# A decoder layer on one core: query and latent-key projections computed with features on partitions, cross scores kept in the row buffer, a norm in two steps, and a last recurrence level by products

## The chip, the core and the metric

One NeuronCore of one Trainium2 chip. The metric is device time in microseconds for one execution of the whole kernel. All arithmetic is f32; large products are made of three f32r matmuls each (high by high, high by low, low by high).

## The reference, cut to what matters

256 tokens, width 2048, one layer. Cut to the parts near the change:

```python
hq, hf, hi, hg, cq, ckv, kr, gate_a, gate_b = split(h @ w_in)
# gated linear recurrence, 16 heads of 128
q = silu(hq);  f = lb + (1 - lb) * sigmoid(hf);  k = 1 - f;  v = hi
o = hgrn2_chunked(q, k, v, log(f))     # o_t = S_t^T q_t,  S_t = diag(f_t) S_(t-1) + k_t^T v_t
o = rmsnorm(o, g_hg_out) * silu(hg)
y_a = o @ w_o_hg
# latent attention, 16 heads, 128 plain and 64 rotary features
q_m = rmsnorm(cq, g_q_lora) @ w_uq;   kv = rmsnorm(ckv, g_kv_lora) @ w_ukv
att = causal_softmax_attention([q_nope, rope(q_rope)], [k_nope, rope(kr)], v_m)
y_b = att @ w_o_mla
merged = sigmoid(gate_a) * y_a + sigmoid(gate_b) * y_b
y = merged @ w_out                      # then norms, residual, SwiGLU, norms, residual
```

## The kernel before, in words

**Stages.** A start phase (to about 277 us) makes the modulated input hT and the latents cT, both transposed (features on partitions) and split in high and low parts. Then a loop over 4 groups of 4 heads (512 columns). Then three 2048-column projections (attention output "om", recurrence output "oh", "out"), and the channel mixing over 11 blocks of 512 hidden columns.

**Chunks.** All weights stream in chunks of 2 x 128 rows by 512 columns (512 KB) through a ring of 4 slots. For chunk c, SP issues the load into `raw` when the low part of chunk c - 4 is done; ScalarE rounds it to `whi` (line 463) when chunk c - 4 is multiplied; VectorE makes `wlo` = raw - whi (line 1220); TensorE multiplies (lines 836 to 838): 2 token tiles x 2 row tiles x 3 products, the activations as the stationary operand and the weights moving, into one of two pairs of PSUM banks. The remaining four banks are the workspaces XA (banks 4, 5) and XB (6, 7).

**The turn.** The group loop is software pipelined and written out by hand over the step t. In a turn i, TensorE multiplies the chunks t = 0 to 7 (values of the recurrence, HI) and 8 to 15 (output gate, HG) of group i, then for group i + 1: t = 16, 17 the query (UQ), 18, 19 the latent key (UK), 20, 21 the rotary query (UR, 256 columns), 22, 23 the value (UV), 24 to 31 the forget gate (HF), 32 to 39 the recurrence query (HQ). Each engine runs over the same t, ScalarE and VectorE up to three chunks ahead of TensorE, and after its chunk work it does what `recur` (group i) and `attention` (group i + 1) have for that t. The first group's attention runs alone ("lead", t from 16), the last group's recurrence runs in a tail: t = 0 to 15, then beside the chunks c of "om", with t = 16 + c.

**Recurrence.** With qT, kT (features on partitions) and bT (running sums of log f), the scores are made level by level, LEVELS = 64, 32, ..., 1. For a level of half length m, POOL subtracts bT at the middle of each block of 2m (`differences`, lines 197, 198), ScalarE exponentiates the tile in place (596), VectorE multiplies the later halves with qT and the earlier halves with kT into zT (1503, 1504), TensorE multiplies each of 8 head tiles with itself (981, t = DECAY[L] - 2, so t = 15 for the last), and VectorE merges the result into pT by a mask (1517). POOL's last difference (193) is for the scores between the two token tiles: TensorE 990 (t = 16), ScalarE's copy to pTx (601, t = 19), which is the first half of qT. Then TensorE's `attend` (862 to 864, t = 18) gives the outputs in XB. ScalarE squares them (607, t = 21). VectorE at t = 20 multiplies the gate (1536), which frees the bank pair that chunk 18 needs, and at t = 22 it reduces the squares (1540), makes mean + eps, waits for POOL's power (789), normalises (1544) and gates (1549).

**Attention.** The query of 16, 17 comes out with tokens on partitions; ScalarE copies it to `stage` (t = 20), TensorE transposes it into XA (845, t = 21), ScalarE copies it to qT (617, t = 24). The key goes through `v` (t = 22), TensorE (t = 24, after the norm has left XB), and to kT (623, t = 27). VectorE rotates the rotary query at t = 23 (1380 to 1386), TensorE transposes it at t = 25 (1014). The scores follow at t = 27 (1026, 1027), softmax, and `attend` at t = 35. `stage` holds the forget gate from t = 35.

**Beside it.** Half-chunks of the modulation matrix are accumulated by VectorE (`ada_piece`, line 1227) at the steps in ADA_TURN, and in "om" at c = 4, 5, 7, 8, 9, 10, 13, ...; SP loads two ahead. In the tail, finished rows are transposed by TensorE (854), raised by ScalarE (`rows_high`, 573) and lowered by VectorE (`rows_low`, 1440 or 1437); chunk c of "om" needs the rows c.

Of the kernel before, what the change touches and what calls it, by code (L numbers as in the profile page):

```python
# [114 lines left out]
def build(nc, x, vectors, consts, masks, positions, ada0, ada1, ada2, ga_bias, post_rows, w_start, w_kr, w_uqn, w_uqr, w_uk, w_uv, w_hf,  # L115
          w_hq, w_hi, w_hg, w_omla, w_ohg, w_out, w_gate, w_up, w_down, out):
    ctx = ExitStack()
    with ctx:
# [29 lines left out]
        pTx = qT[:, 0:HPG]  # L148
        v = sb("v", [P, TT, NW])
# [37 lines left out]
        def differences(eng, L):  # L187
# [7 lines left out]
            b, d = halves(flat(bT), m), halves(d, m)  # L195
            end = b[:, :, 0, m - 1:m].broadcast_to([P, HPG * P // m, m])
# [109 lines left out]
        T_CROSS, T_SUM, T_OG, T_OSQ, T_ON = DECAY[-1] - 2, DECAY[-1], 20, 21, 22  # L306
# [149 lines left out]
        def _(act):  # L456
# [118 lines left out]
            def recur(pl, t, g):  # L575
# [10 lines left out]
                if t + 1 in DECAY:  # L586
# [8 lines left out]
                    dif = tiles(dec[:, L % 2])[:, :, 0, :] if L == len(LEVELS) else dec[:, L % 2]  # L595
# [3 lines left out]
                if t == DECAY[-1] + 1:  # L599
                    act.wait_ge(sig("cross_scored"), g + 1)  # L600
                    nc.scalar.activation(pTx, by_tile(XB)[:, HPG:], ACT.Copy).then_inc(sig("cross_copied"), 1)
# [7 lines left out]
            def attention(pl, t, g, back):  # L609

                if t == 20:
                    from_pair(pl, I_UQ, T_UK - 1, stage[:])
                if t == 22:
                    from_pair(pl, I_UK, T_UR - 1, v[:])
                if t == 24:
                    act.wait_ge(sig("q_transposed"), g + 1)
                    nc.scalar.activation(qT[:], by_tile(XA), ACT.Copy).then_inc(sig("qT_copied"), 1)
                if t == 26:
                    act.wait_ge(sig("k_transposed"), g + 1)
                    from_pair(pl, I_UV, T_HF - 1, v[:])  # L620
                if t == 27:
                    act.wait_ge(sig("k_transposed"), g + 1)
                    nc.scalar.activation(kT[:], by_tile(XB), ACT.Copy).then_inc(sig("kT_copied"), 1)
# [195 lines left out]
        def _(pe):  # L819
# [20 lines left out]

            def transpose_group(src, bank):
# [16 lines left out]
            def attend():  # L858

                for h in range(HPG):  # L860
                    cols = slice(h * P, (h + 1) * P)
                    nc.tensor.matmul(PS[:, XB, cols], pT[:, 2 * h], v[:, 0, cols], start=True, stop=True)
                    nc.tensor.matmul(PS[:, XB + 1, cols], pTx[:, h], v[:, 0, cols], start=True, stop=False)
# [75 lines left out]
            def mix(pl, t):  # L939
# [5 lines left out]
                elif t < T_HF:  # L945
                    i, c = divmod(t - T_UQ, CL)
                    j = i % 2
                    if c == 0:
                        pe.wait_ge(sig("c_low"), j + 1)
                    multiply(pl, I_UQ + i, CL, T_UQ + i * CL, c, c + 1, cT_hi[:, j], cT_lo[:, j],  # L950
                             NW // 2 if I_UQ + i == I_UR else NW)
# [4 lines left out]
            def recur(pl, t, g):  # L956
# [13 lines left out]
                if t + 2 in DECAY[:-1]:  # L970
# [9 lines left out]
                    for i in range(2 * HPG):  # L980
# [12 lines left out]
                if t == T_SUM:  # L993
                    pe.wait_ge(sig(f"level{len(LEVELS) - 1}_merged"), g + 1)
                    pe.wait_ge(sig("cross_copied"), g + 1)
                    attend().then_inc(sig("o_summed"), 1)

            def attention(pl, t, g, back, total):

                if t == 21:  # L1000
                    pe.wait_ge(sig("krT_copied"), 1)
# [895 lines left out]
```

## Time and profile before

| | |
|---|---|
| median of 3 runs | 1898.57 us (1896.83 to 1901.4) |
| the profiled execution's own time | 1899.58 us |
| its span, first to last instruction | 1897.8 us |
| mean granted TensorE clock | 0.991 of full |
| TensorE busy | 1830.3 us (96%) |
| chain that ended last | TensorE 57%, issue 29%, POOL 5%, VectorE 5%, DMA 4%, ScalarE 1% |
| HBM | 423.38 MB by DMA, 223 GB/s in the mean |

Everything comes from one profiled execution. A listed matmul duration reaches from its start to its modelled end and overlaps the next one; the distance between starts is what a matmul costs the queue. In the timeline an f32 matmul that runs in two passes is counted twice ("x16" for 8 instructions). "Idle before" is time in which the engine did nothing, with what ended it. Names: PE is TensorE, PEld its weight loads, DVE VectorE, ACT ScalarE, SP the queue that issues the DMAs.

### The profile page before, as it was taken

To read this page: it belongs to the slowest core of one execution; us is meant where nothing else is said; L and a number is where in the kernel's file an instruction comes from. 1 tells how busy PE (TensorE), PEld (TensorE's weight loads), DVE (VectorE), ACT (ScalarE), POOL (GpSimd) and SP (SyncE) were. 2 spreads that over 40 slices of the span, in tenths; PEclk is the share of its full clock that TensorE was granted. 3 is DMA by queue.
4 is the path that set the end of the run, shared out by engine and by line. 5 is a ranking of instruction groups with operands and counts; after the bars stand their busy time and mean duration, and the time that the engine had idled before them with its cause. 6 is when DMAs were issued, how large, how long until landed. Compare 5 with 4: busy or idle time off the path is not lost.

```text
span 1897.8 us, 24442 instructions
## 1 busy us (share of the span) xinstructions
PE 1830.3 (96%) x8884; PEld 1536.2 (81%) x8884; DVE 1295.4 (68%) x1361; ACT 893.0 (47%) x1007; POOL 107.4 (6%) x76
## 2 busy tenths in 40 slices
PE   3999999999999999999999998999999999999997
PEld 2788888888888888887878877888888888888886
DVE  7899768668668667677677545566656666665557
ACT  5544545645645645644334446444443444343443
POOL 0000000120120120120000000000000000000000
PEclk9999999999999999999999998999999999999999
DMA  9997548646646646546787653666666666665553
GB/s 384 409 363 249 193 160 291 231 156 227 227 155 222 231 155 222 198 148 239 257 309 245 221 189 105 237 223 221 215 233 222 211 226 220 231 210 177 190 191 131
DMA packets 115985, 423.38 MB, mean 223 GB/s; under 512 B 13008, under 2 KB 13392, under 8 KB 115408
## 3 DMA queue, kind: packets, MB, share of 16 engines
q1 hardware_dynamic: 115920, 422.51, 63.4%
q8 instruction: 42, 0.69, 0.1%
q14 instruction: 23, 0.19, 0.0%
HBM read 420.36 MB, written 2.10 MB: 223 GB/s over the span
## 4 chain that ended last, share of the span: by engine, by line
PE 57%; issue 29%; POOL 5%; DVE 5%; DMA 4%; ACT 1%; SPq 0%; POOLq 0%; DVEq 0%; ACTq 0%
PE PS L836 18%; PE PS L838 18%; PE PS L837 18%; POOL dec L197 3%; DMA ada_raw<-in_ada 2%; DVE ada_acc L1227 2%; POOL dec L198 2%; DMA raw<-in_w_start 2%; DVE wlo L1220 1%; PE PS L871 1%; PE PS L1138 1%; PE PS L845 1%; PE PS L896 0%; POOL dec L193 0%; PE PS L854 0%
## 5 line engine op out<-in xcount | busy, mean ns | idle before, releaser
L1220 DVE TENSOR_TENSOR wlo<-raw,whi 128x1024 fp32r<-128x1024 f32 x600 | 731.9, 1222 | 421.8 <-ACT whi L463 420.0
L463 ACT ACTIVATE whi<-raw 128x1024 fp32r<-128x1024 f32 x600 | 630.0, 1053 | 741.1 <-PE PS L838 671.9
L836 PE MATMUL PS<-whi,hT_hi 128*128 128x512 f32 x1792 | 708.5, 395 | 11.2 <-DVE wlo L1220 4.3
L838 PE MATMUL PS<-whi,hT_lo 128*128 128x512 f32 x1792 | 699.5, 390 | 0.0
L837 PE MATMUL PS<-wlo,hT_hi 128*128 128x512 f32 x1792 | 699.0, 390 | 0.0
L836 PEld LDWEIGHTS PS<-whi,hT_hi 128*128 128x128 f32 x1792 | 337.6, 188 | 82.4 <-issue 5.3
L838 PEld LDWEIGHTS PS<-whi,hT_lo 128*128 128x128 f32 x1792 | 337.1, 188 | 71.3
L837 PEld LDWEIGHTS PS<-wlo,hT_hi 128*128 128x128 f32 x1792 | 337.7, 188 | 67.6 <-issue 0.2
L836 PE MATMUL PS<-whi,cT_hi 128*128 128x512 f32 (+1 forms) x592 | 230.9, 390 | 4.9 <-DVE wlo L1220 3.4
L838 PE MATMUL PS<-whi,cT_lo 128*128 128x512 f32 (+1 forms) x592 | 227.9, 385 | 0.0
L837 PE MATMUL PS<-wlo,cT_hi 128*128 128x512 f32 (+1 forms) x592 | 227.7, 385 | 0.0
L1227 DVE SCALAR_TENSOR_TENSOR ada_acc<-ada_raw,csilu,ada_acc 128x512 f32<-128x512 f32 (+1 forms) x185 | 141.2, 763 | 35.4 <-DMA ada_raw<-in_ada 31.8
L836 PEld LDWEIGHTS PS<-whi,cT_hi 128*128 128x128 f32 x592 | 111.7, 189 | 29.2 <-DVE wlo L1220 5.3
L838 PEld LDWEIGHTS PS<-whi,cT_lo 128*128 128x128 f32 x592 | 111.6, 188 | 22.5
L837 PEld LDWEIGHTS PS<-wlo,cT_hi 128*128 128x128 f32 x592 | 111.8, 189 | 21.2
L789 POOL TENSOR_TENSOR stat<-stat,con 128x2 f32<-128x2 f32 (+2 forms) x11 | 12.9, 1175 | 1336.9 <-DVE stat L1279 1321.5
L1392 DVE TENSOR_TENSOR gate<-gate,PS 128x1024 f32<-128x1024 f32 x64 | 78.0, 1219 | 14.5 <-PE PS L838 14.3
L197 POOL TENSOR_TENSOR dec<-bT 128x512 f32<-128x512 f32 x28 | 54.0, 1929 | 413.4 <-DVE bT L1485 338.9
L981 PEld LDWEIGHTS PS<-zT 128*128 128x128 f32 x448 | 54.0, 191 | 1.9
L981 PE MATMUL PS<-zT 128*128 128x64 f32 x448 | 53.0, 271 | 0.0
L1517 DVE COPY_PREDICATED pT<-msk,PS 128x512 f32<-128x512 uint8 x28 | 25.1, 896 | 37.4 <-issue 30.2
L596 ACT ACTIVATE dec<-dec 128x1024 f32<-128x1024 f32 (+1 forms) x32 | 32.1, 1003 | 21.0 <-POOL dec L198 21.0
(222 smaller groups left out, 1054.8 us busy)
## 6 DMA issues: line engine op xcount, KB each, us to landing
ada_raw<-in_ada SPq DMA_DIRECT2D x142, 512.0 KB, 4.9
raw<-in_w_gate SPq DMA_DIRECT2D x88, 512.0 KB, 4.3
raw<-in_w_up SPq DMA_DIRECT2D x88, 512.0 KB, 4.2
raw<-in_w_down SPq DMA_DIRECT2D x88, 512.0 KB, 4.2
raw<-in_w_start SPq DMA_DIRECT2D x80, 512.0 KB, 5.0
raw<-in_w_hf SPq DMA_DIRECT2D x32, 512.0 KB, 4.2
raw<-in_w_hq SPq DMA_DIRECT2D x32, 512.0 KB, 5.2
raw<-in_w_hi SPq DMA_DIRECT2D x32, 512.0 KB, 4.3
```

The costliest lines, as they stand in the source:

```text
L197: eng.tensor_tensor(d[:, :, 1, :], b[:, :, 1, :], end, ALU.subtract)
L198: return eng.tensor_tensor(d[:, :, 0, :], end, b[:, :, 0, :], ALU.subtract)
L463: nc.scalar.activation(whi[:, pl.slot(c), 0:w], raw[:, pl.slot(c), 0:w], ACT.Copy)\
L596: nc.scalar.activation(dif, dif, ACT.Exp).then_inc(sig("decays"), 1)
L836: nc.tensor.matmul(o, hi[:, kt, tok], whi[:, s, cols], start=start, stop=False)
L837: nc.tensor.matmul(o, hi[:, kt, tok], wlo[:, s, cols], start=False, stop=False)
L838: last = nc.tensor.matmul(o, lo[:, kt, tok], whi[:, s, cols], start=False, stop=stop)
L981: last = nc.tensor.matmul(PS[:, XA + L % 4, i * 64:(i + 1) * 64], z[:, i], zt[:, i, :, 1, :], start=True, stop=True)
L1220: nc.vector.tensor_tensor(wlo[:, s, 0:w], raw[:, s, 0:w], whi[:, s, 0:w].bitcast(F32), ALU.subtract)\
L1227: last = nc.vector.scalar_tensor_tensor(out=acc, in0=slot, scalar=csilu[:, a:a + 1], in1=acc, op0=ALU.mult, op1=ALU.add)
L1392: nc.vector.tensor_tensor(dst, dst, banks(2 * p), ALU.add).then_inc(pair_free[p], 1)
L1517: nc.vector.copy_predicated(o, mask.unsqueeze(1).broadcast_to(shape), PS[:, XA + L % 4, :].rearrange("p (i x m) -> p i x m", i=2 * HPG, m=m))\
```

## The change

- The chunks of UQ and UK are multiplied by a new `multiply_columns`: the weights are the stationary operand and the 256 tokens move, so that the result has the features on partitions. ScalarE copies it straight to qT and kT. The transposes of `stage` and `v` at t = 21 and 24, and the two copies behind them, are gone; their waits are put elsewhere.
- The cross scores of the recurrence go to `crossed`, the first half of `stage`, instead of to the first half of qT.
- The last recurrence level (m = 1) is made of one difference, an exponential of half the size, two products on VectorE, of which the second uses the first, and one matmul with ones.
- The norm of the recurrence output is cut in two: reduce and mean + eps at t = 22, the rest at t = 24.
- In the tail `rows_low` of rows 6 and 7 is at c = 5 instead of c = 6.

```diff
+        crossed = stage[:, 0].rearrange("p (h s) -> p h s", s=P)
...
             b, d = halves(flat(bT), m), halves(d, m)
+            if m == 1:
+                return eng.tensor_tensor(dec[:, L % 2, 0:NW], b[:, :, 1, 0], b[:, :, 0, 0], ALU.subtract)
...
-        T_CROSS, T_SUM, T_OG, T_OSQ, T_ON = DECAY[-1] - 2, DECAY[-1], 20, 21, 22
+        T_CROSS, T_SUM, T_OG, T_OSQ, T_OMEAN, T_ON = DECAY[-1] - 2, DECAY[-1], 20, 21, 22, 24
...
@@ ScalarE, recur @@
-                    dif = tiles(dec[:, L % 2])[:, :, 0, :] if L == len(LEVELS) else dec[:, L % 2]
+                    dif = (tiles(dec[:, L % 2])[:, :, 0, :] if L == len(LEVELS) else
+                           dec[:, L % 2, 0:NW] if LEVELS[L] == 1 else dec[:, L % 2])
                     nc.scalar.activation(dif, dif, ACT.Exp).then_inc(sig("decays"), 1)
...
-                    nc.scalar.activation(pTx, by_tile(XB)[:, HPG:], ACT.Copy).then_inc(sig("cross_copied"), 1)
+                    nc.scalar.activation(crossed, by_tile(XB)[:, HPG:], ACT.Copy).then_inc(sig("cross_copied"), 1)
@@ ScalarE, attention @@
                 if t == 20:
-                    from_pair(pl, I_UQ, T_UK - 1, stage[:])
+                    if back is not None:
+                        act.wait_ge(sig("decayed"), back * 8 + 8)
+                    from_pair(pl, I_UQ, T_UK - 1, flat(qT))
                 if t == 22:
-                    from_pair(pl, I_UK, T_UR - 1, v[:])
-                if t == 24:
-                    act.wait_ge(sig("q_transposed"), g + 1)
-                    nc.scalar.activation(qT[:], by_tile(XA), ACT.Copy).then_inc(sig("qT_copied"), 1)
+                    from_pair(pl, I_UK, T_UR - 1, flat(kT))
                 if t == 26:
-                    act.wait_ge(sig("k_transposed"), g + 1)
+                    if back is not None:
+                        act.wait_ge(sig("o_summed"), back + 1)
                     from_pair(pl, I_UV, T_HF - 1, v[:])
-                if t == 27:
-                    act.wait_ge(sig("k_transposed"), g + 1)
-                    nc.scalar.activation(kT[:], by_tile(XB), ACT.Copy).then_inc(sig("kT_copied"), 1)
@@ TensorE @@
+            def multiply_columns(pl, g, c0, c, hi, lo):
+
+                p = pl.pair(g)
+                if c == 0 and not pl.fresh(g):
+                    pe.wait_ge(pair_free[p], pl.freed(g))
+                pe.wait_ge(lo_ready, pl.through(c0 + c))
+                s = pl.slot(c0 + c)
+                for h in range(HPG):
+                    o = PS[:, 2 * p + h // 2, h % 2 * T:(h % 2 + 1) * T]
+                    for k in range(KC):
+                        kt = c * KC + k
+                        cols = slice(k * NW + h * P, k * NW + (h + 1) * P)
+                        start, stop = c == 0 and k == 0 and h % 2 == 0, c == CL - 1 and k == KC - 1
+                        nc.tensor.matmul(o, whi[:, s, cols], hi[:, kt, :], start=start, stop=False, skip_group_check=True)
+                        nc.tensor.matmul(o, whi[:, s, cols], lo[:, kt, :], start=False, stop=False, skip_group_check=True)
+                        last = nc.tensor.matmul(o, wlo[:, s, cols], hi[:, kt, :], start=False, stop=stop,
+                                                skip_group_check=True)
+                last.then_inc(multiplied, 1)
...
+                    if I_UQ + i in (I_UQ, I_UK):
+                        multiply_columns(pl, I_UQ + i, T_UQ + i * CL, c, cT_hi[:, j], cT_lo[:, j])
+                    else:
+                        multiply(pl, I_UQ + i, CL, T_UQ + i * CL, c, c + 1, cT_hi[:, j], cT_lo[:, j],
+                                 NW // 2 if I_UQ + i == I_UR else NW)
@@ TensorE, recur @@
-                    for i in range(2 * HPG):
+                    if m == 1:
+                        last = nc.tensor.matmul(PS[:, XA + L % 4, :], ones, zT[:, L % 2, NW:2 * NW], start=True, stop=True)
+                    for i in range(2 * HPG if m > 1 else 0):
@@ TensorE, attention @@
-                if t == 21:
-                    pe.wait_ge(sig("krT_copied"), 1)
-                    pe.wait_ge(pair_free[pl.pair(I_UQ)], pl.freed(I_UQ) + 1)
-                    transpose_group(stage, XA).then_inc(sig("q_transposed"), 1)
-                if t == 24:
-                    if back is not None:
-                        pe.wait_ge(sig("o_normed"), back + 1)
-                    pe.wait_ge(pair_free[pl.pair(I_UK)], pl.freed(I_UK) + 1)
-                    transpose_group(v, XB).then_inc(sig("k_transposed"), 1)
-                    pe.wait_ge(sig("qT_copied"), g + 1)
...
                 if t == 27:
 
-                    pe.wait_ge(sig("kT_copied"), g + 1)
+                    if back is not None:
+                        pe.wait_ge(sig("o_normed"), back + 1)
+                    pe.wait_ge(sig("krT_copied"), 1)
+                    pe.wait_ge(pair_free[pl.pair(I_UQ)], pl.freed(I_UQ) + 1)
+                    pe.wait_ge(pair_free[pl.pair(I_UK)], pl.freed(I_UK) + 1)
                     pe.wait_ge(sig("qrT_copied"), g + 1)
@@ VectorE, recur @@
+                    if L == len(LEVELS) - 1:
+                        later, products = zT[:, L % 2, 0:NW], zT[:, L % 2, NW:2 * NW]
+                        nc.vector.tensor_tensor(later, halves(flat(qT), 1)[:, :, 1, 0], dec[:, L % 2, 0:NW], ALU.mult)\
+                          .then_inc(sig("q_stepped"), 1)
+                        dve.wait_ge(sig("q_stepped"), g + 1)
+                        nc.vector.tensor_tensor(products, halves(flat(kT), 1)[:, :, 0, 0], later, ALU.mult)\
+                          .then_inc(sig("decayed"), 1)
+                        return
...
-                if t == T_ON:
+                if t == T_OMEAN:
...
-                    rsqrt_of(stat[:, 32:40], P, "o", g)
+                    nc.vector.tensor_scalar(stat[:, 32:40], stat[:, 32:40], 1.0 / P, EPS, ALU.mult, ALU.add)\
+                      .then_inc(sig("o_mean"), 1)
+                if t == T_ON:
+
+                    dve.wait_ge(sig("o_rsqrt"), g + 1)
...
-                for u in {3: (4, 5), 6: (6, 7), 12: (8, 9), 14: (10, 11), 29: (12,), 30: (13,), 31: (14,), 32: (15,)}.get(c, ()):
+                for u in {3: (4, 5), 5: (6, 7), 12: (8, 9), 14: (10, 11), 29: (12,), 30: (13,), 31: (14,), 32: (15,)}.get(c, ()):
```

## Rows read from the trace of the kernel before

**Rows 1.** The page: engines (part 1), modulation products (part 5), their loads (part 6).
```profile
PE 1830.3 (96%) x8884; PEld 1536.2 (81%) x8884; DVE 1295.4 (68%) x1361; ACT 893.0 (47%) x1007; POOL 107.4 (6%) x76
...
L1227 DVE SCALAR_TENSOR_TENSOR ada_acc<-ada_raw,csilu,ada_acc 128x512 f32<-128x512 f32 (+1 forms) x185 | 141.2, 763 | 35.4 <-DMA ada_raw<-in_ada 31.8
...
ada_raw<-in_ada SPq DMA_DIRECT2D x142, 512.0 KB, 4.9
```

**Rows 2.** Who waited for whom, TensorE, 370 to 512.4 us (one turn).
```profile
PE PS L836 <- DVE wlo L1220: 1.2, 2, 1.0
```

**Rows 3.** The same view, 797.2 to 900 us (the last group's recurrence).
```profile
PE PS L836 <- DVE hT_lo L1440: 3.7, 1, 3.7
```

**Rows 4.** Timeline, TensorE, one turn: start us, us, engine, line, operation [idle before].
```profile
408.97 0.39 PE L836 MATMUL PS<-whi,hT_hi 128*128 128x512 f32 x1
...
411.69 1.89 PE L981 MATMUL PS<-zT 128*128 128x64 f32 x16
...
416.25 1.07 PE L990 MATMUL PS<-zT 128*128 128x128 f32 x8
...
420.57 0.49 PE L836 MATMUL PS<-whi,cT_hi 128*128 128x512 f32 x1 [0.48 <-DVE side L1536]
...
428.83 0.28 PE L836 MATMUL PS<-whi,cT_hi 128*128 128x256 f32 x1
...
431.70 1.04 PE L845 MATMUL PS<-con,stage 128*128 128x128 f32 x8
...
435.12 0.39 PE L838 MATMUL PS<-whi,cT_lo 128*128 128x512 f32 x1
436.48 0.50 PE L836 MATMUL PS<-whi,cT_hi 128*128 128x512 f32 x1 [0.97 <-DVE wlo L1220]
...
442.64 1.03 PE L845 MATMUL PS<-con,v 128*128 128x128 f32 x8
...
446.25 0.60 PE L1014 MATMUL PS<-con,zT 128*128 128x128 f32 x4
```

**Rows 5.** Timeline, TensorE's weight loads, a rotary chunk.
```profile
288.50 0.19 PEld L836 LDWEIGHTS PS<-whi,cT_hi 128*128 128x128 f32 x1
```

**Rows 6.** Timeline, TensorE, in the channel mixing.
```profile
1729.51 3.60 PE L1163 MATMUL PS<-gate,con 128*128 128x512 f32 x8
...
1733.18 0.39 PE L837 MATMUL PS<-wlo,hT_hi 128*128 128x512 f32 x1
```

**Rows 7.** Timeline, VectorE, the same turn.
```profile
410.68 0.68 DVE L1504 TENSOR_TENSOR zT<-kT,dec 128x512 f32<-128x512 f32 x1
...
429.44 1.21 DVE L1540 TENSOR_REDUCE stat<-dec 128x8 f32<-128x1024 f32 x1
...
432.60 1.23 DVE L1544 TENSOR_TENSOR dec<-PS,stat 128x1024 f32<-128x1024 f32 x1 [1.75 <-POOL stat L789]
434.07 1.23 DVE L1549 TENSOR_TENSOR mixed<-dec,side 128x1024 f32 x1 [0.24 <-DVE dec L1544]
435.21 1.22 DVE L1220 TENSOR_TENSOR wlo<-raw,whi 128x1024 fp32r<-128x1024 f32 x1
...
438.46 2.36 DVE L1220 TENSOR_TENSOR wlo<-raw,whi 128x1024 fp32r<-128x1024 f32 x2
```

**Rows 8.** Timeline, VectorE, the last group's output norm.
```profile
864.90 1.23 DVE L1544 TENSOR_TENSOR dec<-PS,stat 128x1024 f32<-128x1024 f32 x1 [1.75 <-POOL stat L789]
```

**Rows 9.** Timeline, TensorE, the same stretch.
```profile
863.99 0.39 PE L838 MATMUL PS<-whi,hT_lo 128*128 128x512 f32 x1
868.04 0.50 PE L836 MATMUL PS<-whi,hT_hi 128*128 128x512 f32 x1 [3.66 <-DVE hT_lo L1440]
...
875.25 0.39 PE L836 MATMUL PS<-whi,cT_hi 128*128 128x512 f32 x1
```

**Rows 10.** Busy times, 868.4 to 871.6 us; the granted clock stands before DMA share, GB/s.
```profile
868.40:871.60 3.20, 3.20 (x9) 2.50 (x8) 3.17 (x5) 0.00 (x0) 0.00 (x0) 0.52 0.24 77
```

**Rows 11.** Timeline, ScalarE, the same stretch.
```profile
858.53 1.09 ACT L573 ACTIVATE hT_hi<-PS 128x512 fp32r<-128x512 f32 x2 [2.15 <-PE PS L854]
```

More of the change, by code:

```diff
@@ L856, in transpose_pair, with attend @@
                 return last
-            def attend():
+            def attend(across):
                 for h in range(HPG):
@@ L862, in attend @@
                     nc.tensor.matmul(PS[:, XB, cols], pT[:, 2 * h], v[:, 0, cols], start=True, stop=True)
-                    nc.tensor.matmul(PS[:, XB + 1, cols], pTx[:, h], v[:, 0, cols], start=True, stop=False)
+                    nc.tensor.matmul(PS[:, XB + 1, cols], across[:, h], v[:, 0, cols], start=True, stop=False)
                     last = nc.tensor.matmul(PS[:, XB + 1, cols], pT[:, 2 * h + 1], v[:, 1, cols],
@@ L949, in mix @@
                         pe.wait_ge(sig("c_low"), j + 1)
-                    multiply(pl, I_UQ + i, CL, T_UQ + i * CL, c, c + 1, cT_hi[:, j], cT_lo[:, j],
-                             NW // 2 if I_UQ + i == I_UR else NW)
+                    if I_UQ + i in (I_UQ, I_UK):
[3 more added lines that the diff above has]
+                                 NW // 2 if I_UQ + i == I_UR else NW)
                 else:
@@ L995, in recur @@
                     pe.wait_ge(sig("cross_copied"), g + 1)
-                    attend().then_inc(sig("o_summed"), 1)
+                    attend(crossed).then_inc(sig("o_summed"), 1)
             def attention(pl, t, g, back, total):
-                if t == 21:
-                    pe.wait_ge(sig("krT_copied"), 1)
-                    pe.wait_ge(pair_free[pl.pair(I_UQ)], pl.freed(I_UQ) + 1)
-                    transpose_group(stage, XA).then_inc(sig("q_transposed"), 1)
-                if t == 24:
-                    if back is not None:
-                        pe.wait_ge(sig("o_normed"), back + 1)
-                    pe.wait_ge(pair_free[pl.pair(I_UK)], pl.freed(I_UK) + 1)
-                    transpose_group(v, XB).then_inc(sig("k_transposed"), 1)
-                    pe.wait_ge(sig("qT_copied"), g + 1)
                 if t == 25:
@@ L1039, in attention @@
                     pe.wait_ge(sig("p_copied"), g * 2 + 2)
-                    attend().then_inc(sig("att_summed"), 1)
+                    attend(pTx).then_inc(sig("att_summed"), 1)
                 if t == 39:
```

## The prediction

> **What bounds the kernel now.** First the page's engine totals: TensorE is busy 96% of the span, VectorE 68%, ScalarE 47% [rows 1]. So what counts is whether an edit shortens TensorE's own queue, or a wait of TensorE. Then who waited for whom, for TensorE, around the parts touched. In one turn of the group loop it waits three times: twice for a low part of a weight chunk (wlo, L1220), once for the output gate (side, L1536) [rows 2, 4]. In the last group's recurrence it waits once, for the low rows of L1440, 3.7 us [rows 3]. Then TensorE's timeline, where the start-to-start distance of matmuls is the price of each, since the listed durations overlap [rows 4]; and VectorE's timeline, to see why it was late. I number chunks by the loop variable t of a turn.
>
> **The yardstick.** A chunk of 12 matmuls of 512 columns takes 411.69 - 408.97 = 2.72 us, 0.227 each [rows 4]. The sum is made against the profiled execution's own 1899.58 us (span 1897.8); the median of the runs is 1898.57, 1.0 us lower.
>
> **1. Sixteen transposes a group go (t = 21 and 24).** From the start of the q block at 431.70 to the end of the chunk behind it (last matmul 435.12, plus 0.23) is 3.65 us; less the chunk's 2.72, the block costs 0.93. The k block: 446.25 - 442.64 - 2.72 = 0.89 [rows 4]. Together 1.82, the drag on the chunk behind included; four groups: **-7.3 us**. ScalarE loses its two copies of transposed data (L617, L623): it lies beside other work, worth nothing by itself.
>
> **2. Query and key chunks run with 24 matmuls of 256 columns instead of 12 of 512.** The same columns, twice the weight loads. The rotary chunks already have that width: 24 of them take 431.70 - 428.83 = 2.87 us, 0.12 each [rows 4]. So +0.15 a chunk, 4 chunks a group, 16 in all: +2.4. In each turn one of the four (t = 17) runs while TensorE would wait anyhow: the chunk behind it waits 0.48 for the gate at 420.57 [rows 4], which hangs on ScalarE's copy of the cross scores and so on the cross product of 416.25, not on the chunk between. That gives 0.15 back in three turns: **+1.95 us**. A load is listed with 0.19 [rows 5], yet the 256-column matmuls start 0.12 apart, so the loads are overlapped.
> By the gap formula in the Trainium skill (TensorE: Matmul & The Clock Gate, "Back-to-back issue gap": columns at 2.4 GHz plus 2.5 ns) a chunk would grow by an estimated 0.03 us and this term would be 0.5; the row's 0.12 is above that formula's 0.109, and I go by the row.
>
> **3. The last level's eight products become one.** The block of t = 15: 416.25 - 411.69 - 2.72 = 1.84 us [rows 4]. The new instruction (ones against 512 columns of f32) has four of its kind in L1163: 1733.18 - 1729.51 less one matmul of 0.227 is 3.44, 0.86 each [rows 6]; with 0.05 of drag, 0.91. Gain 0.93, four groups: **-3.7 us**. Bounds: no cheaper than one plain pass (0.227, gain 1.6), no dearer than now (gain 0). Around it: POOL makes one difference instead of two and ScalarE half an exponential, both earlier on the chain; VectorE still makes two products of half the tile, but the second now waits for the first. The nearest such wait of VectorE on itself is 0.24 [rows 7]. The product was ready at 410.68 + 0.68 = 411.36 and used at 411.69, so 0.33 covers 0.24; if not, it costs about 0.1 a turn. The input stride of the two products is as before.
>
> **4. The norm in two steps takes VectorE's stall away.** Now VectorE at t = 22 reduces (429.44), stands 1.75 us for POOL's power (432.60), normalises and gates, and only at 435.21 comes to the low part of chunk 23; the rotation then puts that of chunk 24 at 438.46 [rows 7]. TensorE has ended chunk 22 at 435.35 and reaches 442.64 after two chunks: 7.29 - 5.44 = 1.85 us lost, the slower matmuls after each restart included [rows 4]. After the change, on the same clock: parts 2 and 3 shift TensorE by -0.93 + 0.45 = -0.48 before the place where the q block stood, so chunk 22 starts at 431.2 and chunks 23, 24, 25 are wanted at 433.9, 436.7, 439.4. VectorE: reduce and scale to 430.4, low part of 23 (about 1.15; two are 2.36 [rows 7]) ready 431.5, rotation (438.46 - 435.21 less a low part, 2.1) to 433.6, low part of 24 at 434.8; the norm and gate, 2.6 at t = 24 with POOL done long before, to 437.4; low part of 25 at 438.5. The least slack is 0.9. All 1.85 goes, in three turns: **-5.55 us**. The first group has no such waits, because no recurrence runs beside it.
> The moved waits: scores at t = 27 now stand behind the norm (o_normed), ready about 436 and wanted after 445; ScalarE's value copy at t = 26 waits for o_summed, its query copy at t = 20 for the decays, both done earlier on the same chain. While ScalarE held t = 26 for the key transposes, chunk 27's high part stood behind it; that comes earlier now. SP's loads follow the low parts and are not reordered. POOL's order is the same, one instruction shorter.
>
> **5. The tail.** Rows 6 and 7 are lowered at c = 5, ahead of the reduce; before, behind the whole norm, which begins at 864.90 after 1.75 us for POOL [rows 8]. TensorE, which could have gone on at 863.99 + 0.23 = 864.22, starts at 868.04 [rows 9], and after that pause its granted clock is 0.52 of full, that is the 1.2 GHz level, for some 3.2 us [rows 10], so that two chunks end at 875.25 instead of 864.22 + 5.44 = 869.66: 5.59 us lost [rows 9]. Afterwards ScalarE's high rows (858.53 to 859.6 [rows 11]) let VectorE lower rows 6 and 7 by 860.8, do the modulation piece of c = 5 that now stands behind them (two products of 0.76 [rows 1]), and the low part of chunk 6 by 863.5: 0.7 ahead of 864.22. Chunks 7 and 8 have about 1.0. Then norm and gate at c = 8, its modulation piece and the low part of chunk 9 end near 873.6, when TensorE, three chunks and a block of transposes after 864.22, wants it at 873.3; that new wait with its restart is 0.5. **-5.1 us**. The modulation load for c = 8 waits for the piece of c = 5, now at 862.3; it lands 4.9 us later [rows 1] and is used at 871.
>
> **Sum**: -7.3 + 1.95 - 3.7 - 5.55 - 5.1 = -19.7; 1899.6 - 19.7 = 1879.9, and as the median stands 1.0 lower I say 1879.5.
>
> **Rivals.**
> A. VectorE stays late: the norm's second half at t = 24 delays the next chunks as the first did. For it: VectorE's queue is dense there, slack 0.9. Against: the 1.75 stall goes whatever the order. It returns 5.55: 1885. Chance 0.12.
> B. The tail's wait stays, for chunk 6 or 9: VectorE stands at c = 5 for the high rows with the modulation piece and chunk 6's low part queued behind it. If that passes the pause which brought the lower clock, all of 5.1 returns: 1884.6. Chance 0.08; A and B both, 1890, within these.
> C. Slower: the weight loads of the columns form aren't hidden. Its place is the 16 query and key chunks, 192 more loads; it decides at (19.7 + 1.95) / 192 = 0.11 us a load. At the listed 0.19 [rows 5] it is +36.5 in place of +1.95: 1914. Against: the 256-column rows, load included, at 0.12 [rows 4]; new is only which operand is stationary. Chance 0.03.
> The Trainium skill (TensorE: Matmul & The Clock Gate, Part 3, "What overlaps and what doesn't") says that a weight load overlaps running matmuls only when its row group differs. By that rule this rival would be the forecast; the trace disagrees with it.
> D. The change doesn't do what it says: another wait takes back what the queue sheds, so that TensorE stands where it did (time about 1898). TensorE's few waits in a turn speak against. Chance 0.03.
> E. More gain: the single product at one pass and the gate's wait gone too (-2.7 - 1.5): 1875. Chance 0.05.
> The forecast itself: 0.69.
>
> **Numbers.** Range 1874 to 1887: E below, A or B singly above with two microseconds of run-to-run spread; outside are both together, C and D. About 0.2% (3.8 us) is what a measurement of this kernel can tell from no change. Faster 0.94, same 0.03, slower 0.03.
>
> **What would show it.** Right: no transposes from stage or v at t = 21 and 24 (L845's count down by 64); query and key chunks at 2.87 us; one product at the last level, 0.9 us between its neighbours; no wait of TensorE for wlo in a turn, the 0.48 for the gate still there; in the tail no wait above 1 us and a granted clock at full. Wrong: 256-column matmuls 0.19 apart or more (C); a wlo wait at chunks 23 to 26 (A); a TensorE pause over 3 us or a half clock in the tail (B).

## The result and the profile after

The changed kernel takes 1888.57 us (median of 4 runs, 1886.25 to 1891.49), the kernel before beside it 1899.64 (4 runs, 1896.83 to 1901.4). The ratio is 0.9943, with an interval of 0.993 to 0.9957. It is 11.1 us faster. I had said 20: the direction was right, and the time lies 1.6 us outside the range. The profiled execution took 1891.49 us, the slowest of the four, its span is 1889.7 and its mean granted clock 0.987. So the two profiles compared below lie only 8.1 us apart, and the medians 11.1.

From the page of the kernel after, engine totals and DMA queues ([rows 1] answer to the first line). The second fence is the line of the page before for the same queue:

```profile
PE 1828.1 (97%) x8956; PEld 1542.1 (82%) x8956; DVE 1295.1 (69%) x1361; ACT 885.4 (47%) x999; POOL 102.5 (5%) x72
...
q8 instruction: 60, 0.98, 0.2%
```

```profile
q8 instruction: 42, 0.69, 0.1%
```

Who waited for whom, TensorE, whole span, kernel after: in all, times, longest.

```profile
PE PS L837 <- issue: 5.9, 3, 3.0
PE PS L837 <- DVE wlo L1239: 3.3, 5, 0.8
PE PS L891 <- DVE ada_acc L1246: 3.2, 2, 1.9
PE PS L855 <- DVE side L1563: 1.2, 3, 0.4
```

The waits that I had read are gone: none for wlo in a turn [rows 2], none for the low rows in the tail [rows 3]. But there is one that I had not asked for. "Issue" is time in which TensorE waited for nothing that the profile shows; the kernel before has it once, 3.0 us at the start, the kernel after three times, 5.9 us.

TensorE's timeline after, one turn, against [rows 4]. The product block with ones (L1004; "x2", two passes) starts at 411.82, the query chunk (L855 to L857) runs at 0.12 a matmul, the wait for the gate is 0.38, and from the rotary chunk at 428.38 to the rotation's transposes at 442.18 nothing stands between the chunks:

```profile
411.82 1.02 PE L1004 MATMUL PS<-zT,con 128*128 128x512 f32 x2
412.28 0.69 PE L855 MATMUL PS<-cT_hi,whi 128*128 128x256 f32 x1
...
415.31 0.28 PE L856 MATMUL PS<-cT_lo,whi 128*128 128x256 f32 x1
415.43 0.28 PE L857 MATMUL PS<-cT_hi,wlo 128*128 128x256 f32 x1
415.55 1.06 PE L1015 MATMUL PS<-zT 128*128 128x128 f32 x8
...
419.86 0.38 PE L855 MATMUL PS<-cT_hi,whi 128*128 128x256 f32 x1 [0.38 <-DVE side L1563]
...
428.38 0.28 PE L837 MATMUL PS<-whi,cT_hi 128*128 128x256 f32 x1
...
431.26 0.40 PE L837 MATMUL PS<-whi,cT_hi 128*128 128x512 f32 x1
...
442.18 0.60 PE L1029 MATMUL PS<-con,zT 128*128 128x128 f32 x4
```

VectorE's timeline after, the same turn, against [rows 7]. The reduction is followed by the mean and at once by the low part of chunk 23, and the norm comes at 434.99 with no wait for POOL:

```profile
428.85 1.21 DVE L1567 TENSOR_REDUCE stat<-dec 128x8 f32<-128x1024 f32 x1
430.10 0.17 DVE L1570 TENSOR_SCALAR stat<-stat 128x8 f32<-128x8 f32 x1
430.59 1.23 DVE L1239 TENSOR_TENSOR wlo<-raw,whi 128x1024 fp32r<-128x1024 f32 x1 [0.31 <-ACT whi L466]
...
433.85 1.22 DVE L1239 TENSOR_TENSOR wlo<-raw,whi 128x1024 fp32r<-128x1024 f32 x1
434.99 1.22 DVE L1575 TENSOR_TENSOR dec<-PS,stat 128x1024 f32<-128x1024 f32 x1
```

**Where the time went.** I laid the starts of the first matmul of 596 of the 600 chunks (all but the last four, which another line multiplies) of the two profiled executions side by side, in order. Negative is earlier than before; each row is the change of the difference over its stretch:

| stretch (times of before) | change, us |
|---|---|
| start phase, to 90 us (instructions that the change doesn't touch) | +1.24 |
| lead: four column chunks +0.62, transposes -1.75 | -1.1 |
| first turn, up to its end: level -0.85, columns +0.28, transposes -1.79, norm -1.85 | -4.2 |
| **from the first turn's last product to the next turn's second chunk** | **+3.2** |
| second turn | -4.2 |
| **its end and the third turn's beginning** | **+4.4** |
| third turn, and then out of the loop | -4.2 |
| tail: level -0.87, the wait for the low rows and its clock -5.59 | -6.5 |
| attention output and the stages behind it, from 875 us | +3.2 |
| sum | -8.1, as the spans (1897.8 and 1889.7) |

The parts that I had costed bring -20.2 where I had said -19.7. What is missing was lost in places where the change edits nothing, above all at the two jumps back of the loop. TensorE's timeline there, first the kernel before, with the 16 passes of the one-column sums (L871) that end a turn and the next turn's first chunk:

```profile
495.15 1.84 PE L871 MATMUL PS<-con,ada_acc 128*128 128x1 f32 x16
496.86 0.49 PE L836 MATMUL PS<-whi,hT_hi 128*128 128x512 f32 x1
497.18 0.40 PE L837 MATMUL PS<-wlo,hT_hi 128*128 128x512 f32 x1
```

The same in the kernel after, at the first jump, the second, and at the end of the third turn, where the loop is left and nothing jumps:

```profile
491.08 1.84 PE L891 MATMUL PS<-con,ada_acc 128*128 128x1 f32 x16
494.33 0.49 PE L837 MATMUL PS<-whi,hT_hi 128*128 128x512 f32 x1 [1.42 <-issue]
...
495.52 0.63 PE L838 MATMUL PS<-wlo,hT_hi 128*128 128x512 f32 x1
495.95 0.63 PE L839 MATMUL PS<-whi,hT_lo 128*128 128x512 f32 x1
...
632.48 1.84 PE L891 MATMUL PS<-con,ada_acc 128*128 128x1 f32 x16
635.75 0.79 PE L837 MATMUL PS<-whi,hT_hi 128*128 128x512 f32 x1 [1.42 <-issue]
...
775.16 1.84 PE L891 MATMUL PS<-con,ada_acc 128*128 128x1 f32 x16
776.87 0.49 PE L837 MATMUL PS<-whi,hT_hi 128*128 128x512 f32 x1
```

Busy times of the kernel after behind each jump and behind the third turn (PE, PEld, DVE, ACT, POOL, then granted clock, DMA share, GB/s):

```profile
495.00:499.00 4.00, 4.00 (x12) 3.09 (x11) 2.33 (x5) 3.63 (x8) 0.00 (x0) 0.57 0.02 5
...
636.00:641.00 5.00, 5.00 (x12) 3.86 (x13) 2.93 (x7) 4.00 (x8) 0.00 (x0) 0.50 0.12 35
...
775.00:779.00 4.00, 4.00 (x27) 3.60 (x26) 1.02 (x2) 3.61 (x5) 0.00 (x0) 1.00 0.42 134
```

At each jump TensorE stands 1.42 us, and then its granted clock is 0.57 and 0.50, that is mostly the 1.2 GHz level: 8 and 14 matmuls 0.43 us apart instead of 0.227. And what came in meanwhile stands in the instruction queue: DMA queues between 475 and 780 us, before and then after.

```profile
q8 instruction: 1, 0.02, 0.0%
```

```profile
q8 instruction: 19, 0.31, 0.4%
```

These 18 more are all that the page counts more (60 against 42). 0.31 MB in 19 packets is 16 KB each.

### The profile page after: what moved, and what is told of

Same layout as the page of the kernel before. It is cut to its first block, busy times and chain, and to the rows that moved or that the text cites. A ratio compares the mean times of both kernels' runs of the same rounds, so it can differ in the third digit from the quotient of the medians.

```text
span 1889.7 us, 24569 instructions
## 1 busy us (share of the span) xinstructions
PE 1828.1 (97%) x8956; PEld 1542.1 (82%) x8956; DVE 1295.1 (69%) x1361; ACT 885.4 (47%) x999; POOL 102.5 (5%) x72
## 4 chain that ended last, share of the span: by engine, by line
PE 88%; DVE 5%; DMA 4%; issue 1%; ACT 1%; SPq 0%; POOL 0%; DVEq 0%; ACTq 0%; POOLq 0%
PE PS L837 26%; PE PS L839 26%; PE PS L838 26%; DMA ada_raw<-in_ada 3%; DVE ada_acc L1246 2%; PE PS L1006 2%; DMA raw<-in_w_start 1%; PE PS L891 1%; DVE wlo L1239 1%; PE PS L865 1%; PE PS L855 1%; PE PS L856 1%; PE PS L857 1%; PE PS L1046 1%; PE PS L1045 1%
## 5 line engine op out<-in xcount | busy, mean ns | idle before, releaser
L837 PE MATMUL PS<-whi,cT_hi 128*128 128x512 f32 (+1 forms) x528 | 204.4, 387 | 0.5 <-DVE wlo L1239 0.5
L838 PE MATMUL PS<-wlo,cT_hi 128*128 128x512 f32 (+1 forms) x528 | 203.1, 385 | 0.0
L839 PE MATMUL PS<-whi,cT_lo 128*128 128x512 f32 (+1 forms) x528 | 203.0, 384 | 0.0
L837 PEld LDWEIGHTS PS<-whi,cT_hi 128*128 128x128 f32 x528 | 100.0, 189 | 20.2 <-DVE wlo L1239 1.1
L839 PEld LDWEIGHTS PS<-whi,cT_lo 128*128 128x128 f32 x528 | 99.8, 189 | 19.6
L838 PEld LDWEIGHTS PS<-wlo,cT_hi 128*128 128x128 f32 x528 | 99.9, 189 | 18.9
L200 POOL TENSOR_TENSOR dec<-bT 128x512 f32<-128x512 f32 x24 | 44.3, 1845 | 396.2 <-DVE bT L1504 327.3
L1006 PEld LDWEIGHTS PS<-zT 128*128 128x128 f32 x384 | 46.2, 192 | 1.6
L1006 PE MATMUL PS<-zT 128*128 128x64 f32 x384 | 45.4, 271 | 0.0
L1766 DVE SCALAR_TENSOR_TENSOR gate<-ada_raw,csilu,gate 128x1024 f32<-128x1024 f32 x32 | 40.9, 1279 | 0.0
```

The costliest lines, as they stand in the source:

```text
L200: eng.tensor_tensor(d[:, :, 1, :], b[:, :, 1, :], end, ALU.subtract)
L837: nc.tensor.matmul(o, hi[:, kt, tok], whi[:, s, cols], start=start, stop=False)
L838: nc.tensor.matmul(o, hi[:, kt, tok], wlo[:, s, cols], start=False, stop=False)
L839: last = nc.tensor.matmul(o, lo[:, kt, tok], whi[:, s, cols], start=False, stop=stop)
L1006: last = nc.tensor.matmul(PS[:, XA + L % 4, i * 64:(i + 1) * 64], z[:, i], zt[:, i, :, 1, :], start=True, stop=True)
L1766: nc.vector.scalar_tensor_tensor(out=acc, in0=ada_raw[:, q % 2], scalar=csilu[:, bass.ds(n * 2 + (q // 2 - 2), 1)], in1=acc, op0=ALU.mult, ...
```

## The experiments

**Theory:** the instructions that TensorE runs lie in a store, filled in blocks by DMA, and the jump back is free as long as this store still holds the head of the loop. The change made TensorE's stream longer (in the compiled program the loop begins at its instruction 3235 instead of 3172 and is 1660 long instead of 1625), so that the head no longer lies in it; its blocks are fetched again, TensorE stands, and behind one-column sums plus a stand its clock falls. **Rivals:** one of the five parts brings less than it seems; or VectorE's new order gives the time back elsewhere.

### Shifting the program, first set

The shift is a number of waits that are long fulfilled, ahead of TensorE's first product, where it waits some 25 us for VectorE anyhow. 32 is the number of instructions by which it moves the loop (two of these waits per instruction in the compiled stream); 128 has `range(256)`, and the kernel before moved by 96 has `range(192)`.

```diff
             pe.wait_ge(sig("constants_loaded"), 16)
+            for _ in range(64):
+                pe.wait_ge(sig("constants_loaded"), 16)
```

> A control: the same filling, but 32 instructions, which leaves the changed kernel's loop over 8 blocks. Theory, instruction fetch: 60 or 61 blocks, the idle at the loop's end stays, 1888.6 us. Rival, the filling itself or the new start helps: a time near that of the run with 128.

Measured: 1882.04 us (1880.24 to 1884.01) against 1900.1, ratio 0.991 (0.9895 to 0.9925).

> The changed kernel with 256 waits that are satisfied at once put at the head of TensorE's queue, where it stands idle for the first 30 us anyway. They become 128 instructions (two waits share one), so TensorE's group loop begins half a 256-instruction block later; its 1660 instructions then lie in 7 such blocks instead of 8. Theory, instruction fetch: the changed kernel fetched 60 blocks against 42 before, 18 of them around the two jumps back to the loop's head, where TensorE stood for 1.4 us and more and then ran at half clock, 3.1 and 4.4 us lost. Then this run fetches 42 or 43 blocks, has no such idle at the loop's end, and takes 1888.6 - 7.5 = about 1881 us. Rival, the clock alone: TensorE's clock falls after the sixteen one-column products of t = 39 whatever the fetches do; then the time stays at 1888 and the pauses stay.

Measured: 1882.9 us (1881.78 to 1886.71), ratio 0.9916 (0.9902 to 0.9929).

> The kernel before, with 96 instructions of the same filling: its loop of 1625 instructions then lies in 8 blocks instead of 7, and nothing else changes. Theory, instruction fetch: about 60 blocks instead of 42, idle of 1.4 us or more at the two jumps back, and 3 to 8 us slower than before (1902 to 1907). Rival, the stall belongs to what the change put in the loop: same as before, 1899.6, with 42 or 43 blocks.

Measured: 1898.68 us, ratio 0.9993 (0.9984 to 1.0002): no difference, 42 packets.

The first of these was meant as a control that stays where it was, and the third should have become slower. Both expectations fell: a loop moved *further* back in the program became fast. TensorE's timeline of the kernel after moved by 32, at the first jump:

```profile
491.41 1.84 PE L891 MATMUL PS<-con,ada_acc 128*128 128x1 f32 x16
493.12 0.49 PE L837 MATMUL PS<-whi,hT_hi 128*128 128x512 f32 x1
```

No stand, 42 packets, and no instruction differs but the shift. So the lost time hangs on the place of the loop. A longer program alone doesn't bring it, and neither does any of the changed operations. What fits these results is a rule by blocks: cut the stream in blocks of 256 instructions, with some 64 instructions that aren't in my count ahead of the first (61 to 66 fit the runs); where the loop touches 7 blocks the jump is free, where it touches 8, nine blocks are fetched again at each jump. This rule was made after the runs, so it needed one that it could lose.

### Shifting the kernel before by 32

The same edit as above, on the kernel before. By the rule its loop, 7 blocks where it is, comes to touch 8.

> The kernel before with 32 instructions of filling at TensorE's head, where its loop of 1625 instructions begins at instruction 3204. The five kernels seen so far (loops from 3172, 3235, 3267, 3268, 3363) fit one rule: some 64 instructions stand ahead of the program, a block has 256, and the jump back is free only if the block of the loop's end is at most 6 after the block of its head. By that rule, instruction fetch theory: before from 3172 just fits, before from 3268 fits again, and from 3204 it does not: about 60 blocks, idle at the two jumps back, 3 to 8 us slower than before (1903 to 1908). Rival, the stall needs the changed loop: 42 blocks, same as before (1900.1).

Measured: 1906.38 us (1904.41 to 1908.23) against 1900.1, ratio 1.0036 (1.0022 to 1.0049). TensorE's timeline at both jumps, and the page's line:

```profile
496.40 1.84 PE L871 MATMUL PS<-con,ada_acc 128*128 128x1 f32 x16
500.08 0.49 PE L836 MATMUL PS<-whi,hT_hi 128*128 128x512 f32 x1 [1.83 <-issue]
...
642.40 1.84 PE L871 MATMUL PS<-con,ada_acc 128*128 128x1 f32 x16
646.16 0.49 PE L836 MATMUL PS<-whi,hT_hi 128*128 128x512 f32 x1 [1.92 <-issue]
```

```profile
q8 instruction: 60, 0.98, 0.2%
```

The kernel before with nothing but a shift shows the whole pattern: 60 packets, two stands, a lower clock behind the first, 6.3 us slower. Busy times behind the two jumps (granted clock before DMA share and GB/s):

```profile
501.00:504.00 3.00, 3.00 (x9) 2.36 (x8) 2.01 (x4) 2.92 (x6) 0.00 (x0) 0.51 0.00 0
646.00:650.00 4.00, 3.84 (x17) 3.17 (x18) 2.00 (x4) 4.00 (x9) 0.00 (x0) 1.00 0.05 15
```

Chunk by chunk the first jump costs it 3.5 us, the second 2.05. At the second no matmul is slow, although the same 1.84 us of one-column products and a stand of 1.92 us lie ahead of it.

### Halving the sums ahead of the jump

Theory: of the loss at a jump, the part behind the stand comes from the clock, which falls because the stand follows 1.84 us of one-column products. Half of these are moved to t = 36; the loop stays in 8 blocks.

```diff
+                if t == 36:
+                    pe.wait_ge(ada_step, total - ADA_N)
+                    sum_rows(ada_sum[0], XA, 0)
                 if t == 39:
                     pe.wait_ge(ada_step, total)
-                    for r, acc in enumerate(ada_sum):
-                        last = sum_rows(acc, XA, r * HPG)
-                    last.then_inc(sig("ada_summed"), 1)
+                    sum_rows(ada_sum[1], XA, HPG).then_inc(sig("ada_summed"), 1)
```

> The changed kernel, its loop where it was, with the sixteen one-column products of t = 39 cut in two: the first eight at t = 36, the other eight at t = 39. The jump back then comes after 0.9 us of them instead of 1.8. Theory: the fetch stall (1.4 us, 60 blocks) stays, but the clock, which fell after 1.8 us of such products and 1.4 us of standing still together, does not fall, or for less: 2 x 1.4 us stay and about 1.6 and 2.9 us come back, 1888.6 - 4.5 = about 1884. Rival, the standing alone takes the clock: 1888.6 and half clock after both jumps.

Measured: 1886.89 us (1884.26 to 1889.96), ratio 0.9938 (0.9922 to 0.9953), 60 packets. TensorE's timeline at the two jumps, and the windows:

```profile
492.59 0.94 PE L891 MATMUL PS<-con,ada_acc 128*128 128x1 f32 x8
494.79 0.49 PE L837 MATMUL PS<-whi,hT_hi 128*128 128x512 f32 x1 [1.25 <-issue]
...
499.00 0.39 PE L839 MATMUL PS<-whi,hT_lo 128*128 128x512 f32 x1 [0.75 <-issue]
...
635.69 0.49 PE L837 MATMUL PS<-whi,hT_hi 128*128 128x512 f32 x1 [1.56 <-issue]
```

```profile
495.00:499.00 4.00, 3.25 (x15) 2.52 (x14) 0.82 (x1) 3.99 (x8) 0.00 (x0) 1.00 0.30 115
636.00:641.00 5.00, 5.00 (x23) 4.04 (x22) 2.21 (x5) 5.00 (x10) 0.00 (x0) 1.00 0.20 76
```

The stands stay, the clock stays at full. Against the kernel after, chunk by chunk, the first jump costs 0.8 us less (2.65 less at the chunks behind the sums; against that stand 0.95 for the half that is now paid at t = 36 and 0.9 for the second stand at 499.00), the second 2.6 less. The medians differ by 1.7 only, less than expected, and the two sets of runs overlap; the profiles compared are the slowest of one set and the fastest of the other. The clock is the evidence here, and it isn't much: with all 16 passes ahead of a stand it fell at three of four jumps (both of the kernel after, the first of the kernel before moved by 32), with 8 passes at none of two. That the sums and the stand bring the lower clock together is likely, and not shown.

### Both cures

Moved by 32, with the sums halved there and also in the attention output and the recurrence output (half at c = 18, half at c = 23).

> The changed kernel with the loop moved by 32 instructions, and the one-column products of the modulation sums in two halves also in the turn (t = 36 and 39) and in the two projections after it (c = 18 and 23). After the move alone the clock still fell in some executions beside the sums of c = 23 (VectorE's pieces came 1.2 us late there), for 1 to 2.5 us. Theory: that goes, 1882.0 - 1 to 2 = 1880.5 us. Rival: the halves cost two more switches of form, 4 to 6 times 0.1 us, and the clock is free of them: 1882 to 1882.5.

Measured: 1880.03 us (1878.93 to 1880.76) against 1900.1, ratio 0.9894 (0.9879 to 0.991). It beats the kernel before and the kernel after, and its spread is the smallest of all. Against the kernel moved by 32 alone the median is 2.0 us lower, as the theory says; but the two sets of runs touch, and the spans of the two profiled executions are the same (1878.8 and 1878.5 us, with a start phase 1.9 us later in the first). What the halves are worth is not shown.

### One part at a time

The norm in two steps and the rows at c = 5, alone on the kernel before:

```diff
-        T_CROSS, T_SUM, T_OG, T_OSQ, T_ON = DECAY[-1] - 2, DECAY[-1], 20, 21, 22
+        T_CROSS, T_SUM, T_OG, T_OSQ, T_OMEAN, T_ON = DECAY[-1] - 2, DECAY[-1], 20, 21, 22, 24
...
-                    rsqrt_of(stat[:, 32:40], P, "o", g)
+                    nc.vector.tensor_scalar(stat[:, 32:40], stat[:, 32:40], 1.0 / P, EPS, ALU.mult, ALU.add)\
+                      .then_inc(sig("o_mean"), 1)
+                if t == T_ON:
+                    dve.wait_ge(sig("o_rsqrt"), g + 1)
...
-                for u in {3: (4, 5), 6: (6, 7), ...
+                for u in {3: (4, 5), 5: (6, 7), ...
```

> The kernel before with only the norm in two steps and rows 6 and 7 lowered at c = 5. By the prediction's parts 4 and 5 it takes 1.85 us out of each of three turns and 5.1 us out of the tail: 1899.6 - 10.6 = 1889 us. But TensorE's key transposes at t = 24 still wait for the norm, which ends later, so a turn may gain less. Rival A of the prediction (VectorE stays late): about 5 us less gain, 1894.5 us.

Measured: 1893.57 us (1891.83 to 1894.58), ratio 0.9966 (0.9952 to 0.9979), so -6.5 in the medians, nearer to the rival's number than to the theory's. Chunk by chunk each turn gives 1.85 and the tail 5.55, 11.1 in all and as the theory has it. Its profiled execution is only 6.0 us shorter than that of before, because it lost time elsewhere: 3.3 us up to the end of the start phase, which no edit touches, and 1.6 in the attention output.

The last level alone on the kernel before (the m = 1 branches of the diff, nothing else):

> The kernel before with only the last recurrence level by products. By the prediction 0.93 us in each of four groups: 1900.1 - 3.7 = 1896.4 us, the block at t = 15 0.9 us between its neighbours instead of 1.8, TensorE's waits for VectorE unchanged. Rival: VectorE was late already, so the queue that gets shorter only waits longer for the low parts (L1220) in the turns: 1899 to 1900 us and longer waits there.

Measured: 1895.04 us (9 runs), ratio 0.9975 (0.9966 to 0.9985): -5.1, so the rival falls. Chunk by chunk it is -0.86 a group, 3.4 in all (-1.25 ahead of chunk 16, +0.39 ahead of the next); for the rest of the 5.1 no cause was found. VectorE's two chained products make no wait longer (1.0 for wlo, as in [rows 2]).

All but the norm and the rows: the kernel after, moved by 32, with the norm in one place (t = 22) and rows 6, 7 at c = 6 again.

```diff
-        T_CROSS, T_SUM, T_OG, T_OSQ, T_OMEAN, T_ON = DECAY[-1] - 2, DECAY[-1], 20, 21, 22, 24
+        T_CROSS, T_SUM, T_OG, T_OSQ, T_OMEAN, T_ON = DECAY[-1] - 2, DECAY[-1], 20, 21, 22, 22
...
-                for u in {3: (4, 5), 5: (6, 7), ...
+                for u in {3: (4, 5), 6: (6, 7), ...
```

> The changed kernel with its loop moved by 32 instructions (7 blocks, no refetch), but with the norm in one step at t = 22 and rows 6 and 7 lowered at c = 6, as before. Against the changed kernel moved by 32 (1882.0) this gives the norm's worth beside the other parts. Parts additive: 1882.0 + 10.6 = 1892.6 us. Rival: without the q block TensorE asks for chunk 23's low part 0.9 us sooner, so the stall of VectorE costs a turn 1.85 + 0.9 + some tenths, three turns 3 us more: 1895 to 1896 us, and waits of TensorE for L1239's line of 3 us a turn instead of 1.2.

Measured: 1890.74 us (1889.7 to 1893.32) against 1900.25, ratio 0.9954 (0.9941 to 0.9968), 8.7 behind the whole change moved by 32. TensorE's timeline of this kernel, one turn:

```profile
435.27 0.50 PE L837 MATMUL PS<-whi,cT_hi 128*128 128x512 f32 x1 [1.73 <-DVE wlo L1241]
...
438.53 0.50 PE L837 MATMUL PS<-whi,hT_hi 128*128 128x512 f32 x1 [0.25 <-DVE wlo L1241]
```

The wait for chunk 23 is 1.73 us instead of 0.97 [rows 4]: without the q block TensorE comes earlier to a low part that comes no earlier. So by the chunk starts the two parts are not additive: beside the transposes' removal the norm's split is worth 2.57 a turn, beside the transposes it is 1.85. With 5.5 in the tail that is 13 us, of which the medians show 8.7, less than either expectation. The spans differ by 10.2: the start phase was 1.0 later in the profile of the faster kernel, and 2.1 are lost again from the attention output on, where the faster kernel waits at the sums of c = 23.

The columns alone: the kernel of the last run with the old last level, moved by 64 (loop in 7 blocks).

> The kernel before with only the query and key chunks by columns (and the cross scores in the row buffer), the loop placed so that it needs no refetch. By the prediction's parts 1 and 2: -7.3 + 1.95 = -5.35, 1900.1 - 5.4 = 1894.7 us. Rival, as the run beside it: the norm in one step holds VectorE, so that the 0.9 a turn of the q block turns into waiting: 1897.5 us. Second rival, rival C of the prediction, loads not hidden: above 1930 us.

Measured: 1895.92 us (11 runs), ratio 0.9976 (0.9967 to 0.9985): -4.3. That lies between the theory and the first rival. The same wait of 1.73 for chunk 23 is there, and by the chunk starts a turn gives 0.7 where transposes and columns give 1.5 beside the norm in two steps. If the weight loads weren't hidden, this kernel would be some 35 us slower than measured (192 loads at 0.19, an estimate from [rows 5]).

The runs by the rule, with 64 instructions ahead of the count, numbers of blocks from (place + 64) / 256:

| kernel | loop from, to | in blocks | blocks touched | packets | stands at the jumps |
|---|---|---|---|---|---|
| before | 3172, 4797 | 12.64 to 18.99 | 7 | 42 | none |
| after | 3235, 4895 | 12.89 to 19.37 | 8 | 60 | 1.42, 1.42 |
| after moved by 32 | 3267, 4927 | 13.01 to 19.50 | 7 | 42 | none |
| after moved by 128 | 3363, 5023 | 13.39 to 19.87 | 7 | 43 | none |
| before moved by 96 | 3268, 4893 | 13.02 to 19.36 | 7 | 42 | none |
| before moved by 32 | 3204, 4829 | 12.77 to 19.11 | 8 | 60 | 1.83, 1.92 |
| sums halved | 3235, 4896 | 12.89 to 19.38 | 8 | 60 | 1.25, 1.56 |
| columns alone, moved | 3299, 4987 | 13.14 to 19.73 | 7 | 43 | none |

The four others (norm alone, last level alone, all but the norm, both cures) have 42 packets each and no stand at the jumps. Another loop agrees: in the channel mixing TensorE runs again and again through some 620 products and loads, far fewer than 7 blocks, and the instruction queue brings nothing from 1255 to 1747 us of the kernel after.

## Why the prediction was wrong

- **Part 1, transposes, -7.3:** right, -1.75 in the lead and -1.79 in each turn, -7.1. The forgotten point is that it hangs on part 4: alone, part 1 would have lost some 0.7 a turn to the norm's stall (2.57 less 1.85). Since part 4 came along, it didn't show.
- **Part 2, columns, +1.95:** +1.46. The chunk that I called free (t = 17) is free, and t = 16 takes only 0.01 more too (0.09 in the kernel with the columns alone), which I can't explain. The row's 0.12 a matmul holds, at 415.31 to 415.43 and everywhere.
- **Part 3, last level, -3.7:** 0.86 a group instead of 0.93, -3.4. VectorE on itself costs nothing.
- **Part 4, norm, -5.55:** right, 1.85 in each turn, no wlo wait left.
- **Part 5, tail, -5.1:** -5.59. The clock stays at full and the new wait for chunk 9 (0.5) doesn't come.
- **The sum, -19.7,** is -20.2 in the stretches that it speaks of.

The step that failed is not a term but one that is missing, in part 2, which reads "The same columns, twice the weight loads" and prices that lengthening of TensorE's stream by the time between two matmuls and by nothing else. 63 instructions ahead of the loop and 35 in it make the loop touch 8 blocks. Of the kernel after this costs 3.2 + 4.4 = 7.6 us in the profiled execution; in the medians the shift by 32 gives 6.5 back (1888.57 to 1882.04, of two sets of runs whose kernels before differ by 0.5). I never looked at the instruction queue of the kernel before. Its single packet between 475 and 780 us, where TensorE runs twice through the 1625 instructions of the loop, would have shown that they were held in the store, and that this is a state that can be lost.

The rest, 2.5 us between the 1882.0 of the moved kernel and my 1879.5, has no one cause that I could show. Some of it is the base: I reckoned from a median of 1898.57, and the same kernel beside the later runs took 1900.1, from which my sum gives 1880.4. And two stretches vary from execution to execution by more than that. The start phase was 0.4 to 3.8 us later in every other profile than in that of before, the kernel before moved by 96 (0.4) and by 32 (1.2) among them. And the stretch of the attention output around its sums at c = 23 stood between -3.7 (before moved by 96, no instruction changed) and +3.2 us (the kernel after, the worst of all). There TensorE waits for VectorE's modulation pieces, now that it comes 11 us earlier, and then its clock falls; its timeline in the kernel after:

```profile
910.68 2.78 PE L891 MATMUL PS<-con,ada_acc 128*128 128x1 f32 x16 [1.26 <-DVE ada_acc L1246]
913.32 0.77 PE L837 MATMUL PS<-whi,cT_hi 128*128 128x512 f32 x1
913.89 0.63 PE L838 MATMUL PS<-wlo,cT_hi 128*128 128x512 f32 x1
```

12 matmuls at the lower clock follow. The kernel before has 8 at the same chunk, the kernel before moved by 96 and the kernel after moved by 32 have none, so the clock comes and goes without an edit. With the sums halved there it wasn't seen, in one profile. The wait is another matter: it is 0.7 to 1.5 us in all six profiles whose tail is the shorter one (rows at c = 5), and 0 to 0.13 in five of the six others (1.87 in the kernel before moved by 32). So about a microsecond of what part 5 gives is likely taken back here by a producer that comes no earlier, and the prediction ended at the tail and didn't look. A sum to a fraction of a microsecond against one execution was finer than the yardstick.

**The rivals.** A and B are false (no such wait). C is false: the 256-column matmuls start 0.12 apart beside loads of 0.19, and the kernel with the columns form alone is faster than before. The rule of the page that I cited beside it is not seen here. E is false: the product isn't one pass (0.86), and the gate's wait of 0.38 stays. D, "another wait takes back what the queue sheds", to which I gave 0.03, had the right form and the wrong size: 7.6 us of 20, at a place where only the instruction stream could tell of it. The chance that something outside the priced stretches takes back a third was what the range left out.

## What to carry to other kernels

A loop on an engine has a size and a place in the instruction stream, and both can cost. Where an edit adds or removes instructions in or ahead of a loop, count the packets of the instruction queue before and after: if they rise by many, look at the first instruction behind the jump, and move the loop by some instructions before judging the edit. Two savings behind the same late producer aren't additive. And a stand can bring the lower clock with it, which at the two jumps here of the kernel after cost 1.6 and 2.9 us more, beside stands of 1.42.

## What was not expected of the hardware

- The stand at a jump back is 1.25 to 1.92 us, 9 blocks of 16 KB are fetched again for each (18 for two jumps), and a shift of 32 instructions decides: 1906.4 against 1900.1 us, and 1888.6 against 1882.0.
- The Trainium skill (Runtime: NRT & Kernel Launch, "Instruction fetch mechanics") gives TensorE's store 2,048 instructions, refilled in blocks of 16 KiB or 256 instructions. The packets here agree with the block (0.98 MB in 60). A loop over 7 blocks that is kept and one over 8 that isn't would agree with a store of 8 blocks, one of which is being filled ahead; that is a guess, since how far it reads ahead was not measured.
- The same section says that a taken branch out of the current window of two pages brings a stall. A stall there is; but the window for TensorE is wider than two pages: the kernel before jumps back over 1625 instructions, 6.3 blocks, and goes on without a pause (495.15 plus the sums' 1.7, to 496.86).
- With the sums halved a second stand of 0.75 us shows 4 us behind the jump. It lies in the stretch in which the blocks are fetched again; what it waits for isn't shown.
- Left open: why 9 blocks and not one come again for each jump, what the 61 to 66 instructions ahead are, and whether the loops of the other engines do the same; no run moved those.
